# Constants, modulation set-up and the transposes of x as one list; four weight tiles of the merge on the ring's common slots

## The chip, the cores and the metric

The kernel runs on one core of one Trainium2 chip. The metric is the device time of one execution in microseconds (us), here the median of several executions. Everything is float32.

## The reference, cut to what matters

A transformer block over 512 tokens of width 1024, followed by two further layers and a small context stream. The part that the change touches is the input side of the first block: `x` is projected by one wide matrix `w_in`, four branches (three-scale window attention, indexed sparse attention, an RWKV-7 recurrence, a Mamba-2 scan) each give 256 columns, and these are merged under gates:

```
merged = sum over n of sigmoid(x @ w_gates[n]) * (branch_n @ w_branch[n])
y      = layer_norm(alpha * x + merged @ w_out)
```

Two sets of constants play a part. An identity matrix serves the transposes on TensorE. `na_mask` is a 16-wide window mask that the neighbourhood attention of the later layers reads. Beside the branches, the kernel computes the modulation of the later layers: `silu(c) @ w_ada + b_ada`, for two condition vectors `c` and `c_ctx`.

## The kernel before

**Stages.** The program is a sequence of blocks. A block gives each engine its own instruction list, and all engines meet at a barrier at its end. Most blocks are built by `products` (L233) from a list of groups. A group is a run of matmuls into one PSUM bank and the step that empties it on VectorE ("v"), ScalarE ("s") or GpSimd ("g"). Each engine works through its part of the list in the list's order, and `extra` adds instructions ahead of the list on SyncE and GpSimd.

**The start.** Three blocks follow one another. `layer_constants` (L545) builds the identity, ones, epsilons, the causal mask and the window mask on GpSimd. The window mask goes to DRAM and comes back spread over 128 partitions (L585, L587), and the block ends when it is back. `Ada.__init__` (L2666) then loads `c`, `c_ctx` and the bias `b_ada` on SyncE, fills `cs` and `pick` on GpSimd, and applies Silu on ScalarE; its block ends when `b_ada` has landed. `load_x` (L593) loads all of x (2 MB) in one transfer, behind it the first four weight tiles, and transposes x in eight groups of four 128x128 transposes into `xT`. The block after it (`branch_a_in`) starts with x times the first tile of `w_in`.

**Weights.** `Weights` (L167) holds the whole program's weight tiles, mostly 2 MB each, in one list in order of use. Each tile has a slot of a ring: `slots[i]` says how many slots tile i may choose from, and it takes the one whose last tile is oldest. `RING` is 4, `DEEP` is 5; slot 4 (`deep_ring_more`) exists only from the stage "deep" on, after the branches. `Weights.load` runs on SyncE in every `products` block. It issues transfers in the list's order, each behind a wait for the last group that used the slot before, and it stops at the first tile whose slot does not exist yet or whose slot's last user belongs to a later block:

```
            if self.slot[i] >= len(self.bufs):
                break
            if self.prior[i] is not None:
                if self.prior[i] not in self.last_group:
                    break
                sp.wait_ge(self.groups_done, self.last_group[self.prior[i]])
```

**The end of branch D and the merge.** The block `d_in` (in `branch_d`, L1463) multiplies x with the last tiles of the branches; the last four modulation tiles (`w_ada`) are used there too. Then come the convolution (`mamba_conv`), the block `d_rows` and the scan. A further block turns y into `oT`. The stage "deep" opens slot 4, and `merge` (L1770) starts. For each branch n it uses three tiles: two of the gates (`w_in`) and one of `w_branch`, 12 in all. The gates' product is made from seven half-size products (`seven`, L1835). Its first two (`one`, `two`) take x and the tiles as they are. The third needs a sum of rows of x (four `row_sums`, L1812, on VectorE) and a difference of weight columns (`right`, on VectorE, which waits for both tiles).

**Semaphores.** A stage that closes puts its semaphores on a list. When more than 100 are on it, `Signals.close` (L122) clears them all with instructions on GpSimd and all engines meet at one more barrier (L125, L126). This happens twice: after the convolution of branch D, and before the first layer of the second block.

## Time and profile before

| | |
|---|---|
| median of 3 runs | 4184.86 us (4181.7 to 4187.54) |
| profiled execution, its own time | 4185.21 us |
| its span, first to last instruction | 4183.3 us |
| TensorE (PE) busy | 3772.9 us, 90% of the span |
| VectorE (DVE) busy | 1747.9 us, 42% |
| ScalarE (ACT) busy | 759.7 us, 18% |
| GpSimd (POOL) busy | 170.5 us, 4% |
| mean granted TensorE clock | 0.945 of full speed |
| weights and data moved | 575.73 MB, mean 138 GB/s |

In the rows, PE is TensorE's matmuls and PEld its weight loads; SPq is a transfer issued by SyncE (SP), at the time of its issue; PEq, POOLq are the engines' sequencers. `L342` is a line of the kernel, often of a helper. "us to landing" is the time from a transfer's issue to its semaphore. An fp32 matmul over 512 columns appears as several records.

### The profile page before, as it was taken

How to read it: one execution, taken by the hardware profiler on the slowest of the kernel's cores; microseconds unless marked ns; L12 is line 12 of the kernel's file. 1: busy time of each engine (PE TensorE's matmuls, PEld its weight loads, DVE VectorE, ACT ScalarE, POOL GpSimd, SP SyncE). 2: the span in 40 equal slices, each digit the busy share in tenths (PEclk: the TensorE clock that was granted, in tenths of full speed). 3: DMA queues.
4: the chain of work that ended last, by engine and by line, in shares of the span. 5: the costliest groups of instructions: out<-in, count | busy, mean ns of one | idle time of the engine just before them, and what ended most of it. 6: DMA issues, size and time to landing. Idle time of an engine off the chain costs nothing. (4 is left out here: it accounts for less than half of the span.)

```text
span 4183.3 us, 38449 instructions
## 1 busy us (share of the span) xinstructions
PE 3772.9 (90%) x14796; PEld 2136.3 (51%) x14796; DVE 1747.9 (42%) x3047; ACT 759.7 (18%) x1696; POOL 170.5 (4%) x377
## 2 busy tenths in 40 slices
PE   7988777799878989999777999999998899999999
PEld 3653664444534435455433545458744555447844
DVE  0118743444523211111144555355446556345546
ACT  0212211111112201000122434010001354111000
POOL 1001000000010000000020200000000300000000
PEclk9989777799889999999988999999999999999999
DMA  7543001223266588888753110132222201122221
GB/s 294 180 160 112 1 4 51 91 101 122 93 245 271 205 331 352 343 340 343 309 190 107 41 61 21 71 111 81 81 81 86 103 21 61 61 81 81 81 81 60
DMA packets 197672, 575.73 MB, mean 138 GB/s; under 512 B 24548, under 2 KB 34580, under 8 KB 184232
## 3 DMA queue, kind: packets, MB, share of 16 engines
q1 hardware_dynamic: 177608, 517.31, 33.0%
q10 hardware_dynamic: 12000, 29.46, 2.0%
q0 software_dynamic: 7888, 26.53, 1.8%
q8 instruction: 120, 1.97, 0.2%
q14 instruction: 56, 0.46, 0.0%
HBM read 541.54 MB, written 31.73 MB: 137 GB/s over the span
## 5 line engine op out<-in xcount | busy, mean ns | idle before, releaser
L342 PE MATMUL ps<-out_sums 128*128 128x256 f32 (+1 forms) x1152 | 333.6, 450 | 2.3 <-issue 2.3
L342 PEld LDWEIGHTS ps<-out_sums 128*128 128x128 f32 x1152 | 218.7, 190 | 114.2 <-issue 94.5
L342 PE MATMUL ps<-mixers_xT,ring 128*128 128x512 f32 (+1 forms) x480 | 209.2, 594 | 0.9 <-PEq L272 0.9
L342 PE MATMUL ps<-ring,layers_hT 128*128 128x512 f32 x416 | 186.7, 607 | 21.8 <-PEq L126 11.3
L2262 PE MATMUL ps<-ring,mixers_xT 128*64 128x512 f32 x416 | 184.0, 599 | 3.8 <-issue 2.8
L2263 PE MATMUL ps<-ring,mixers_xT 128*64 128x512 f32 x416 | 186.5, 605 | 0.0
L342 PE MATMUL ps<-ring,out_hidden 128*128 128x512 f32 x384 | 167.4, 592 | 0.0
L342 PEld LDWEIGHTS ps<-mixers_xT,ring 128*128 128x128 f32 (+1 forms) x480 | 88.6, 187 | 115.8 <-issue 115.6
L342 PE MATMUL ps<-ring,deep_c_hT 128*128 128x512 f32 (+2 forms) x352 | 132.6, 534 | 11.8 <-PEq L272 11.0
L342 PEld LDWEIGHTS ps<-ring,layers_hT 128*128 128x128 f32 x416 | 79.6, 194 | 123.1 <-issue 119.1
L342 PE MATMUL ps<-out_hidden 128*128 128x512 f32 x288 | 125.7, 593 | 6.2 <-issue 6.2
L342 PE MATMUL ps<-layers_hT,ring 128*128 128x256 f32 x512 | 115.3, 387 | 5.1 <-ACT out_rms_rs L2592 5.1
L342 PEld LDWEIGHTS ps<-ring,out_hidden 128*128 128x128 f32 x384 | 73.0, 190 | 91.0 <-issue 90.9
L2262 PEld LDWEIGHTS ps<-ring,mixers_xT 128*64 128x64 f32 x416 | 56.2, 138 | 123.1 <-issue 123.1
L2300 DVE TENSOR_TENSOR moe_h<-moe_sg,ps 128x512 f32<-128x512 f32 x16 | 11.0, 688 | 253.4 <-PE ps L2263 253.4
L342 PE MATMUL ps<-ring,layers_yT 128*128 128x512 f32 x256 | 112.5, 592 | 0.0
L342 PEld LDWEIGHTS ps<-layers_hT,ring 128*128 128x128 f32 x512 | 99.4, 195 | 19.7 <-issue 5.5
L342 PE MATMUL ps<-ring,mixers_xT 128*128 128x512 f32 (+2 forms) x320 | 100.1, 470 | 8.0 <-DVE ab_qk L336 6.3
L342 PEld LDWEIGHTS ps<-ring,deep_c_hT 128*128 128x128 f32 x352 | 65.1, 193 | 77.0 <-issue 74.5
L430 PE MATMUL ps<-mla_kT,mla_qT 96*128 96x512 f32 (+1 forms) x256 | 96.8, 502 | 8.1 <-ACT mla_S L444 6.6
L342 PE MATMUL ps<-ring,ctx_ins 128*128 128x512 f32 (+1 forms) x232 | 98.1, 581 | 5.5 <-ACT ctx_ins L3239 3.3
L2262 PE MATMUL ps<-ring,moe_hT 128*64 128x512 f32 x192 | 88.0, 613 | 16.5 <-ACT moe_hT L334 7.6
(894 smaller groups left out, 6490.0 us busy)
## 6 DMA issues: line engine op xcount, KB each, us to landing
ring<-in_w_ff SPq DMA_DIRECT2D x44, 2048.0 KB
ring<-in_w_in SPq DMA_DIRECT2D x40, 2048.0 KB
ring<-in_e_up SPq DMA_DIRECT2D x27, 2048.0 KB
ring<-in_e_gate SPq DMA_DIRECT2D x25, 2048.0 KB
ring<-in_e_down SPq DMA_DIRECT2D x25, 2048.0 KB
ring<-in_w_ada SPq DMA_DIRECT2D x24, 2048.0 KB
ring<-in_w_out SPq DMA_DIRECT2D x8, 2048.0 KB
deep_ring_more<-in_e_gate SPq DMA_DIRECT2D x8, 2048.0 KB, 7.8
```

Source lines behind the costliest of these rows:

```text
L342: last = pe.matmul(out, lhsT, rhs, start=(j == 0), stop=(j == len(pairs) - 1))
L430: last = pe_.matmul(bank[:, e * BANK + c0:e * BANK + c0 + n], q, k, start=True, stop=True)
L2262: pe.matmul(bank[0:HALF, :], left(k)[:, 0:HALF], wa[:, k, cols], **ends)
L2263: last = pe.matmul(bank[HALF:P, :], left(k)[:, HALF:P], wb[:, k, cols], **ends)
L2300: lambda eng, bank, link, i=i: eng.tensor_tensor(h[:, i, :], sg[:, i, :], bank, ALU.mult),
```

## The change

1. The constants that the first blocks need, the modulation's set-up and the transposes of x become one block. SyncE's list is: x, then `c`, `c_ctx` and `b_ada` (two transfers), then the first four weight tiles. GpSimd makes the identity first and raises a semaphore `ident`, on which TensorE's first transpose waits beside `x_in`. The Silu becomes a group on ScalarE at the head of the list. GpSimd ends with a wait for `b_ada`.
2. x lands in `mixed` (the space of `oT`) and no longer in a buffer of its own.
3. The window mask is made in the block `branch_a_in`, behind the 16 zero-writes to `y_slot` that GpSimd issues there.
4. Of the merge's 12 tiles, the first four take their slot among the 4 common ones.

```
-        slots = [RING] * len(tiles)
+        slots = [RING] * (len(tiles) + RING)
...
-            with Stage(nc, "const") as sc:
-                layer_constants(M, sc)
...
 def load_x(M, st):
-    x_rows = st.sb("x_rows", [P, TT, D])
+    sig, ada = st.sig, M.ada
+    x_rows = M.mixed[:, :, :, :].rearrange("p i k n -> p (i k n)").rearrange("p (t d) -> p t d", t=TT)
 
     def sync(sp):
         sp.dma_start(x_rows[:, :, :], M.A["x"].rearrange("o (t p) d -> p (o t) d", p=P)
                      ).then_inc(sig["x_in"], 16)
+        ada.load(sp, M.A)
+
+    def constants(pool):
+        first_constants(M, st, pool)
+        ada.constants(pool)
+        pool.wait_ge(ada.sig["ada_b"], 16 * LAYERS)
...
     def first_pe(pe, bank):
+        pe.wait_ge(sig["ident"], 1)
         pe.wait_ge(sig["x_in"], 16)
         return first(pe, bank)
     gs[0].pe = first_pe
-    products(M, "xT", gs, extra={"sync": sync})
+    products(M, "xT", [group(None, ada.silu, "s")] + gs, extra={"sync": sync, "gpsimd": constants})
...
+            small = sa.sb("small", [WIN, 3, 2 * WIN])
...
                 for b in range(NE // 2, NBLK):
                     pool.dma_start(spare[b], z).then_inc(sa.sig["zeroed"], 16)
+                window_mask(M, small, sa.sig, pool)
                 pool.wait_ge(sa.sig["zeroed"], SPARE * 16)
...
+    def load(self, sp, A):
+        sp.dma_start(self.c[:, 0, :], A["c_2"]).then_inc(self.sig["ada_in"], 16)
+        sp.dma_start(self.c[:, 1, :], A["c_ctx_2"]).then_inc(self.sig["ada_in"], 16)
+        for l in range(LAYERS):
+            sp.dma_start(self.b[:, l, :], A["b_ada_2"][l]).then_inc(self.sig["ada_b"], 16)
...
+    def silu(self, act, _, link):
+        act.wait_ge(self.sig["ada_in"], 32)
+        act.wait_ge(self.sig["ada_zero"], 1)
+        return act.activation(self.cs[:, :, 0:2].rearrange("p k s -> p s k"), self.c[:, :, :], ACT.Silu)
```

`first_constants` and `window_mask` are the two halves of the old `layer_constants`; their instructions are the old ones.

SyncE at the start of the program. Before, two barriers and a wait for `b_ada` stand ahead of the transfer of x:

```order
L2675 UNCONDITIONAL_BRANCH [waits barrier_Pool_Activation_PE_DVE_SP_release]
L2677 DMA mixers_ada_c<-in_c 128x8
L2678 DMA mixers_ada_c<-in_c_ctx 128x8
L2680 DMA mixers_ada_b<-in_b_ada 128x48 x2
L2674 UNCONDITIONAL_BRANCH [waits mixers_ada_b]
L273 UNCONDITIONAL_BRANCH [waits barrier_Pool_Activation_PE_DVE_SP_release]
L599 DMA x_x_rows<-in_x 128x4x1024
L200 DMA ring<-in_w_in 128x8x512
L200 DMA ring<-in_w_ada 128x8x512 x2
L200 DMA ring<-in_w_in 128x8x512
```

And with the change:

```order
L273 UNCONDITIONAL_BRANCH [waits barrier_Pool_Activation_PE_DVE_SP_release]
L607 DMA mixers_oT<-in_x 128x4x1024
L2694 DMA mixers_ada_c<-in_c 128x8
L2695 DMA mixers_ada_c<-in_c_ctx 128x8
L2697 DMA mixers_ada_b<-in_b_ada 128x48 x2
L200 DMA ring<-in_w_in 128x8x512
L200 DMA ring<-in_w_ada 128x8x512 x2
L200 DMA ring<-in_w_in 128x8x512
```

x is the first transfer, and the four small ones stand between it and the first weight tile.

SyncE from the last tiles of `d_in` to the start of the merge, before:

```order
L200 DMA ring<-in_w_ada 128x8x512 [waits groups_done,d_conv_loads]
L200 DMA ring<-in_w_ada 128x8x512 [waits groups_done]
L272 UNCONDITIONAL_BRANCH
L273 UNCONDITIONAL_BRANCH [waits barrier_Pool_Activation_PE_DVE_SP_release]
L1537 DMA scratch_L<-ssm_dtl 4x512
L1539 DMA ssm_L_all<-scratch_L 128x2048 [waits xT_moved_v]
L272 UNCONDITIONAL_BRANCH [waits xT_moved_s]
L273 UNCONDITIONAL_BRANCH [waits barrier_Pool_Activation_PE_DVE_SP_release] x2
L200 DMA deep_ring_more<-in_w_in 128x8x512
L200 DMA ring<-in_w_in 128x8x512 [waits groups_done]
L200 DMA ring<-in_w_branch 128x2x1024 [waits groups_done]
L200 DMA ring<-in_w_in 128x8x512 [waits groups_done] x2
```

And with the change (the first of these rows is the second `w_ada` tile above):

```order
L200 DMA ring<-in_w_ada 128x8x512 [waits groups_done]
L200 DMA ring<-in_w_in 128x8x512 [waits groups_done] x2
L200 DMA ring<-in_w_branch 128x2x1024 [waits groups_done]
L200 DMA ring<-in_w_in 128x8x512 [waits groups_done]
L272 UNCONDITIONAL_BRANCH
L273 UNCONDITIONAL_BRANCH [waits barrier_Pool_Activation_PE_DVE_SP_release]
L1555 DMA scratch_L<-ssm_dtl 4x512
L1557 DMA ssm_L_all<-scratch_L 128x2048 [waits xT_chain_v]
L272 UNCONDITIONAL_BRANCH [waits xT_chain_s]
L273 UNCONDITIONAL_BRANCH [waits barrier_Pool_Activation_PE_DVE_SP_release] x2
L200 DMA deep_ring_more<-in_w_in 128x8x512
```

The merge's first four transfers have moved from the merge's block into `d_in`; only the fifth stands at the merge's start. From there on SyncE's list has the same transfers in the same order, with the tile that takes slot 4 moved by one (in each five, the fifth and no longer the first).

GpSimd where the semaphores are cleared for the first time, after the convolution's masks of branch D. Before:

```order
L1502 MEMSET d_conv_pre 128x4x3 [waits d_conv_masks]
L272 UNCONDITIONAL_BRANCH [waits d_conv_masks]
L125 ISA [waits barrier_Pool_Activation_PE_DVE_SP_gather]
L125 ISA x3
L322 UNCONDITIONAL_BRANCH [waits barrier_Pool_Activation_PE_DVE_SP_gather] x5
```

And with the change:

```order
L1520 MEMSET d_conv_pre 128x4x3 [waits d_conv_masks]
L272 UNCONDITIONAL_BRANCH [waits d_conv_masks]
L125 ISA [waits barrier_Pool_Activation_PE_DVE_SP_gather]
L125 ISA x5
L322 UNCONDITIONAL_BRANCH [waits barrier_Pool_Activation_PE_DVE_SP_gather] x5
```

The clearing has six instructions and no longer four; at the second place, before the second block's first layer, it has five and no longer four. Both places stay where they were.

## Rows read from the trace of the kernel before

**Rows 1.** The page, part 1: busy time, share of the span, instructions of each engine.

```profile
PE 3772.9 (90%) x14796; PEld 2136.3 (51%) x14796; DVE 1747.9 (42%) x3047; ACT 759.7 (18%) x1696; POOL 170.5 (4%) x377
```

**Rows 2.** Timeline, 0 to 28 us: start, duration, instruction, [idle before <-releaser].

```profile
0.81 0.20 POOL L554 MEMSET ident<- 128x128 f32 x1 [0.29 <-POOLq L4115]
...
7.43 0.55 POOL L587 DMA_DIRECT2D na_mask<-mask  x1 [1.39 <-DMA mask<-const_small]
...
10.95 0.90 SPq L2680 DMA_DIRECT2D mixers_ada_b<-in_b_ada  x2
...
13.65 0.39 SPq L599 DMA_DIRECT2D x_x_rows<-in_x  x1
14.09 0.50 SPq L200 DMA_DIRECT2D ring<-in_w_in  x1
...
21.70 5.48 PE L395 MATMUL ps<-ident,x_x_rows 128*128 128x128 f32 x32 [21.70 <-DMA x_x_rows<-in_x]
...
23.28 3.69 SPq L200 DMA_DIRECT2D ring<-in_w_in  x1
23.71 0.60 ACT L334 ACTIVATE mixers_xT<-ps 128x512 f32<-128x512 f32 x1 [11.36 <-PE ps L395]
...
28.12 27.71 PE L342 MATMUL ps<-mixers_xT,ring 128*128 128x512 f32 x64 [0.94 <-PEq L272]
```

**Rows 3.** Stretch after x has landed: ..., PEclk, DMA share, GB/s (last columns).

```profile
21.70:24.00 2.30, 2.30 (x11) 2.30 (x12) 0.69 (x1) 0.29 (x1) 0.00 (x0) 1.00 1.05 387
```

**Rows 4.** DMA issues: tensor, count, KB each, median us from issue to landing.

```profile
x_x_rows<-in_x SPq DMA_DIRECT2D x1, 2048.0 KB, 8.0
...
mixers_ada_b<-in_b_ada SPq DMA_DIRECT2D x2, 24.0 KB, 1.9
...
mixers_ada_c<-in_c SPq DMA_DIRECT2D x1, 4.0 KB, 1.8
mixers_ada_c<-in_c_ctx SPq DMA_DIRECT2D x1, 4.0 KB, 1.6
...
c_first_cols<-in_c_rk SPq DMA_DIRECT2D x1, 1.0 KB, 1.8
```

**Rows 5.** Timeline, end of d_in to the merge's first products.

```profile
684.07 1.95 PE L2717 MATMUL ps<-mixers_ada_pick,mixers_ada_rows 128*128 128x2 f32 x16
...
686.54 0.47 DVE L1556 TENSOR_SCALAR d_dt_s<-ssm_dt_raw,ssm_small 4x512 f32<-4x512 f32 x1 [0.32 <-PEq L272]
...
708.91 1.21 DVE L1580 TENSOR_TENSOR_SCAN ssm_dtl<-d_dt_one,d_dt_s 4x512 f32<-4x512 f32 x1
...
712.25 1.94 PE L395 MATMUL ps<-ident,ssm_xbc 128*128 128x128 f32 x8 [26.23 <-PEq L126]
...
762.70 1.94 PE L395 MATMUL ps<-ident,ssm_y 128*128 128x128 f32 x8 [8.33 <-PEq L1682]
...
765.59 1.22 DVE L1816 TENSOR_TENSOR merge_rows<-mixers_xT 128x1024 f32<-128x1024 f32 x1 [1.07 <-PEq L272]
...
766.59 3.44 SPq L200 DMA_DIRECT2D ring<-in_w_branch  x1
...
778.82 16.13 PE L342 MATMUL ps<-deep_ring_more,mixers_xT 128*128 128x512 f32 x32 [14.17 <-DMA ring<-in_w_in]
778.87 2.29 DVE L1863 TENSOR_TENSOR merge_right<-ring,deep_ring_more 128x2048 f32<-128x2048 f32 x1 [8.53 <-DMA ring<-in_w_in]
...
791.62 0.69 DVE L1881 TENSOR_TENSOR merge_sg<-merge_p,ps 128x512 f32<-128x512 f32 x1 [8.13 <-PE ps L342]
```

**Rows 6.** Stretches at the merge's start, columns as in rows 3.

```profile
778.00:783.00 5.00, 4.18 (x5) 1.85 (x6) 4.09 (x2) 0.00 (x0) 0.00 (x0) 0.50 1.03 395
...
783.00:784.00 1.00, 1.00 (x3) 0.38 (x2) 0.49 (x1) 0.00 (x0) 0.00 (x0) 0.94 1.05 385
```

**Rows 7.** Waits of PE, 1186 to 2090 us: total us, times, longest.

```profile
PE ps L2262 <- DMA deep_ring_more<-in_e_down: 5.7, 3, 2.5
...
PE ps L2262 <- DMA ring<-in_e_down: 3.7, 2, 2.3
```

More of the change, by code:

```diff
@@ new lines, in first_constants, with fill, keep @@
+def first_constants(M, st, pool):
+    link = Chain(pool, st.sig["made"])
+    def fill(ap, value):
+        link(pool.memset(ap, value))
+    def keep(ap, pattern, fill_value, op):
+        link(pool.affine_select(out=ap, in_=ap, compare_op=op, fill=fill_value, base=0, pattern=pattern,
+                                channel_multiplier=1))
+    fill(M.ident[:, :], 0.0)
+    keep(M.ident[:, :], [[-1, P]], 1.0, ALU.not_equal)
+    pool.sem_inc(st.sig["ident"], 1)
+    fill(M.ones[:, :], 1.0)
+    fill(M.eps[:, :], EPS)
+    fill(M.ln_eps[:, :], LN_EPS)
+    fill(M.causal[:, :], 0.0)
+    keep(M.causal[:, :], [[-1, P]], NEG, ALU.is_ge)
@@ new lines, in window_mask, with keep, window @@
+def window_mask(M, small, sig, pool):
+    nc, link = M.nc, Chain(pool, sig["windows"])
+    def keep(ap, pattern, base, cm, fill_value):
+        link(pool.affine_select(out=ap, in_=ap, compare_op=ALU.is_ge, fill=fill_value, base=base,
+                                pattern=pattern, channel_multiplier=cm))
+    link(pool.memset(small[:, :, :], 0.0))
+    def window(kind, c0, c1, low):
+        m = small[:, kind, c0:c1]
+        if low:
+            keep(m, [[1, c1 - c0]], c0, -1, NEG)
+        else:
+            keep(m, [[-1, c1 - c0]], WIN - 1 - c0, 1, NEG)
+    window(0, 0, 2 * WIN, True)
+    window(0, WIN + 8, 2 * WIN, False)
+    window(1, 0, 2 * WIN, True)
+    window(1, 0, 2 * WIN, False)
+    window(2, 0, 8, True)
+    window(2, WIN, 2 * WIN, False)
+    mask16 = nc.dram_tensor("mask16", [WIN, 6 * WIN], F32).ap()
+    pool.dma_start(mask16, small[:, :, :].rearrange("p a n -> p (a n)")).then_inc(sig["mask_out"], 16)
+    pool.wait_ge(sig["mask_out"], 16)
+    pool.dma_start(M.na_mask[:, :, :].rearrange("p a n -> p (a n)"),
+                   bass.AP(mask16.tensor, 0, [[6 * WIN, WIN], [0, ROWS], [1, 6 * WIN]])
+                   ).then_inc(sig["mask_in"], 16)
+    pool.wait_ge(sig["mask_in"], 16)
@@ new lines, in __init__, with constants @@
+        self.c, self.sig = st.sb("ada_c", [P, 2, DK]), sig
+    def load(self, sp, A):
[3 more added lines that the diff above has]
+            sp.dma_start(self.b[:, l, :], A["b_ada_2"][l]).then_inc(self.sig["ada_b"], 16)
+    def constants(self, pool):
+        link = Chain(pool, self.sig["ada_pool"])
+        pool.memset(self.cs[:, :, :], 0.0).then_inc(self.sig["ada_zero"], 1)
+        link(pool.memset(self.pick[:, :], 0.0))
+        for q in range(4):
+            link(pool.affine_select(out=self.pick[:, :], in_=self.pick[:, :], compare_op=ALU.not_equal,
+                                    fill=1.0, base=-32 * q, pattern=[[-1, 2]], channel_multiplier=1))
```

64 lines of the change are left out of this document (removed).

## The prediction

> **What bounds the kernel now.** I read the page first. TensorE is busy for 3772.9 us, 90% of the span [rows 1], and no other engine comes near; so a change counts only where it fills a stretch in which TensorE stands idle. Then I read the timeline at the two places that the diff touches. At the start the reader is to see that TensorE has no work for 21.70 us, and that what ends this wait is the transfer of x, issued only at 13.65 [rows 2]: two blocks of small work stand ahead of it, one up to about 10 us (the window mask's way through DRAM, last issue at 7.43), and one for the loads of c and b_ada. At the merge the reader is to see 14.17 us of idle TensorE that end with a weight tile [rows 5]. Behind both places the matmuls run densely, so time won there moves the rest of the program forward.
>
> **The start: x is issued earlier.** In the changed order the transfer of x is SyncE's first instruction behind the first barrier. The trace has no SyncE row there, but GpSimd's first constant behind the same barrier starts at 0.81 [rows 2], and I take this for SyncE as well. x then goes out 13.65 - 0.81 = 12.84 us earlier. It has an empty queue in both kernels, so it takes the same 8.05 us to TensorE's first transpose (21.70 - 13.65, 8.0 in the row of landings [rows 4]): the transposes start at 8.86. The identity costs nothing, since GpSimd makes it by about 1.5 us. The transposes and their emptying take as long as before, 28.12 - 21.70 = 6.42 us, so the first product with weights could start at 15.28. **-12.84 us.**
>
> **The start: what stands behind x.** Four small loads now lie between x and the first weight tile. The tile before was issued 0.44 us behind x. Its 2.1 MB at 387 GB/s [rows 3] take 5.4 us after x, which lands at 21.70, so it was there at about 27.1 to 27.2, some 0.9 us before 28.12, where TensorE asked for it. The cost of the small loads in a queue that is never empty is not in the trace. From below it is nothing, as they fit into those 0.9 us. From above: SyncE issues such loads 0.45 us apart (two in 0.90 [rows 2]), and the fifth of a series of 1 KB loads issued so still lands in 1.8 us [rows 4], so one keeps the queue for no more than 0.45 us; four make 1.8, less 0.9 of slack, 0.9 us. The issue of the block's last weight tile gives the same bound: it ended at 23.28 + 3.69 = 26.97, 1.1 us before the next block, and moves by at most 1.8. I take **+0.4 us**, the middle, as the ends are near each other. The rest is covered. The Silu waits for c, which lands within a microsecond or two behind x (at 9 to 11), and ScalarE's first emptying comes at 23.71 - 12.84 = 10.87; a Silu that is late by one microsecond is made up in the idle gaps between the four copies. GpSimd's wait for b_ada ends at about 11, four microseconds before the block does. Without this cover each microsecond would count in full.
>
> A rule of the Trainium skill speaks against this order. "DMA: Bandwidth & Descriptors", section "Measured (HBM→SBUF, 128 partitions, SWDGE, issued from GpSimd)", gives about 10.5 ns for each packet however small; four loads of 128 packets would then hold the queue for an estimated 5.4 us and not 1.8, and the sum below would end 4.1 us later. The rows on hand disagree: loads issued 0.45 us apart would pile up, and they do not.
>
> **The window mask** moves behind 16 zero-writes of GpSimd in the next block. That block is dense with matmuls (its first run is 27.7 us long [rows 2], and many follow), GpSimd has nothing else in it, and the mask is read only by the later layers: nothing.
>
> **The merge.** SyncE now issues the first four tiles in d_in, each behind the last group of a slot's previous user. Those are the third-last modulation tile, the last tile of w_in, and the two last modulation tiles, whose products end by about 684 us. All 7 MB at 387 GB/s are in by about 702, 60 us before use. The block that empties the transposes of y ends by 765.59 [rows 5], where VectorE starts on the merge; TensorE starts there too, not at 778.82. That is **-13.2 us** of its 14.17; 1 us is the barrier and stays. Is anything else late in its place? The first two products need only x and the tiles. The third needs a row sum and the first weight difference; VectorE's four sums last until 778.87 - 8.53 = 770.34 and two differences of 2.29 us end at 775, while TensorE comes to the third product only 16 us after its start, at 781.6, and VectorE's first emptying follows TensorE by 791.62 - 778.82 = 12.8 us, at 778.4. So nothing is late, and the merge stays bound by TensorE. The fifth tile is issued at 765.6 and is wanted for the second branch, as before.
>
> **What is put into d_in.** SyncE's last wait there is for the last modulation products, which end in PSUM at about 684.2; behind it one more issue. The block's other work goes on until 686.0 (684.07 + 1.95) and the next starts at 686.54 [rows 5]. An issue takes 0.4 us with room in the queue. At the merge's start, with two tiles issued, the third was held for 3.44 us [rows 5]; as much here would end at 688 and cost 1.3 us. In d_in the queue is emptier by then, so I take nothing, and keep 1.3. The transfers run on beside VectorE's convolution; VectorE's row sum and differences ran beside transfers at the merge too [rows 5], and I take it that nothing is stretched.
>
> **Clearing semaphores** has two more instructions at one place and one more at the other. Around the first place VectorE ends at 710.12 and TensorE starts at 712.25 [rows 5], 2.1 us. An ordinary barrier leaves 0.3 (686.54 [rows 5]), so four instructions and a second barrier take 1.8 us, at most 0.45 each. Three more cost 0 to 1.35 us; I take **+0.4**, since part of the 1.8 is the barrier.
>
> **The clock at the merge.** The granted clock was 0.50, the lower level of 1.2 GHz, until 783, 4.2 us after the products began [rows 6]. With the earlier start TensorE's eight transposes at 762.70 come just before. I let the clock rise 4.2 us after the start of the products again: nothing. If the transposes count, it rises at about 766.9, and 2.9 us of half speed are saved, 1.45 us.
>
> **Slots from there on.** The merge and the experts rotate through five slots in both kernels, each tile waits for the user five tiles back, and SyncE's order is the same: nothing.
>
> **Sum.** -12.84 + 0.4 - 13.2 + 0.4 = -25.2 us. The profiled execution took 4185.21 us, so 4160.0 us; it stands 0.35 above the median of the three runs shown, which is no difference.
>
> **The rivals.**
> - *The small loads hold the queue.* In the worst case each takes its whole landing time in turn: 1.8 + 1.6 + 1.9 + 1.9 = 7.2 us [rows 4], less 0.9 of slack, 6.3 and not 0.4. The time would be 4165.9. Against it is the series that did not pile up; for it, that none was ever behind a full queue. 0.09. The packet rule of "DMA: Bandwidth & Descriptors" in the Trainium skill would land between this and the forecast, at 4164.1.
> - *The transposes count for the clock.* 4160.0 - 1.45 = 4158.5. For it: they are TensorE work less than a microsecond before the products. Against: the whole scan, with TensorE busy, left the clock low. 0.10.
> - *Only one of the two halves pays.* At the merge, tiles issued early don't help if a second wait was hidden behind the first; then 4160.0 + 13.2 = 4173.2. The same size results if x, as the program's very first transfer, came 12 us late. The order of SyncE speaks against the first, landings of 1.6 to 1.8 us for the first transfers of the program against the second. 0.06.
> - *Slower: the shifted fifth slot starves the experts.* There weights arrive only just in time: TensorE waits for e_down in five places, 9.4 us in all, at most 2.5 us each [rows 7]. If the shift made one tile of each of the 16 pairs of experts late by those 2.5 us, it would cost 40 us: 4200. It turns slower by over 8.4 us from 33.6 / 16 = 2.1 us a pair. Against it: each tile still waits for the user five tiles back, in the same order. 0.02.
> - *The change doesn't do what it says*: tiles held until the merge's block. The listed order excludes it for the merge, and x is first in its list. No chance of its own.
>
> **How the numbers follow.** The forecast has 0.73. A measurement of this kernel can tell about 0.2% from no change, 8.4 us, here below 4176.5 us. All cases but the last and a remainder for the unforeseen lie below that: faster 0.97, same 0.01, slower 0.02. The bounds of the costs: at best -12.84 - 13.2 - 1.45 = -27.5 (4157.7), at worst -12.84 + 0.9 - 13.2 + 1.3 + 1.35 = -22.5 (4162.7). The runs shown scatter by 3 us to either side, and the rival with the held queue is taken in: 4155 to 4167 us.
>
> **What would show it.** In the new profile: x issued near 0.8 and the first transpose near 8.9; the first weight product at 15.3 to 16.2, with a wait for the ring if the small loads cost something; the next block of GpSimd at the same time. The block d_in should be followed by the convolution about 12.4 us earlier than before, at 674, and not later; the merge's first product at about 753.5, with 1 us of idle before it and no wait for a tile; from there to the end every stage some 25 us earlier. A wait of TensorE for w_in at the merge, or more than 9.4 us of waits for e_down, would show me wrong; so would a first transpose later than 10 us.

## The result, and the profile after

| | before | changed |
|---|---|---|
| median, first measurement | 4186.2 us (4181.7 to 4191.12, 4 runs) | 4161.9 us (4157.03 to 4166.67, 4 runs) |
| ratio, 95% interval | | 0.9945 [0.9932, 0.9957] |
| median, second measurement (below, *after_again*) | 4184.47 us (4179.93 to 4194.59, 11 runs) | 4155.87 us (4154.18 to 4164.43, 6 runs) |
| ratio, 95% interval | | 0.9933 [0.992, 0.9946] |
| profiled execution | 4185.21 us, span 4183.3 | 4163.72 us, span 4160.9 |

The kernel is faster by 0.55% and 0.67%, 24 and 29 us. The forecast was 4160.0 with a range of 4155 to 4167.

The page after, part 1, answers to [rows 1]: the work is the same, and TensorE's busy time has not shrunk but grown by 4.1 us, within a span shorter by 22.4.

```profile
PE 3777.0 (91%) x14796; PEld 2137.9 (51%) x14796; DVE 1747.7 (42%) x3047; ACT 758.7 (18%) x1696; POOL 170.5 (4%) x377
```

The start of the changed kernel, from the timelines of SyncE, TensorE and ScalarE (start, duration, instruction, idle before); it answers to [rows 2].

```profile
0.81 0.44 SPq L607 DMA_DIRECT2D mixers_oT<-in_x  x1
...
3.38 0.46 SPq L200 DMA_DIRECT2D ring<-in_w_in  x1
...
10.89 3.71 SPq L200 DMA_DIRECT2D ring<-in_w_in  x1
...
9.13 5.50 PE L395 MATMUL ps<-ident,mixers_oT 128*128 128x128 f32 x32 [9.13 <-DMA mixers_oT<-in_x]
15.57 27.71 PE L342 MATMUL ps<-mixers_xT,ring 128*128 128x512 f32 x64 [0.94 <-PEq L272]
...
9.39 0.23 ACT L2710 ACTIVATE mixers_ada_cs<-mixers_ada_c 128x16 f32<-128x16 f32 x1 [4.75 <-DMA mixers_ada_c<-in_c_ctx]
...
14.67 0.60 ACT L334 ACTIVATE mixers_xT<-ps 128x512 f32<-128x512 f32 x1 [0.28 <-PE ps L395]
```

x goes out at 0.81 and the first product with weights starts at 15.57 and not at 28.12: 12.55 us won. The idle before it is the barrier's 0.94 in both kernels, so no weight tile was late. What ends this block is ScalarE: its last emptying of a transpose ends at 15.27 (14.67 + 0.60), and the product follows 0.30 us later. Before the change it was the same, with the last emptying at 27.82 and the product at 28.12:

```profile
27.22 0.60 ACT L334 ACTIVATE mixers_xT<-ps 128x512 f32<-128x512 f32 x1 [0.27 <-PE ps L395]
```

SyncE's last weight load was issued at 14.60 (10.89 + 3.71), 0.67 us before ScalarE was done.

From the clearing of the semaphores to the merge, the timelines of TensorE, SyncE and VectorE; they answer to [rows 5].

```profile
696.31 1.21 DVE L1598 TENSOR_TENSOR_SCAN ssm_dtl<-d_dt_one,d_dt_s 4x512 f32<-4x512 f32 x1
...
699.94 1.94 PE L395 MATMUL ps<-ident,ssm_xbc 128*128 128x128 f32 x8 [26.51 <-PEq L126]
...
750.25 1.94 PE L395 MATMUL ps<-ident,ssm_y 128*128 128x128 f32 x8 [8.33 <-PEq L1700]
753.28 15.80 PE L342 MATMUL ps<-ring,mixers_xT 128*128 128x512 f32 x32 [1.09 <-PEq L272]
...
669.91 0.37 SPq L200 DMA_DIRECT2D ring<-in_w_branch  x1
671.63 0.37 SPq L200 DMA_DIRECT2D ring<-in_w_in  x1
...
753.09 0.38 SPq L200 DMA_DIRECT2D deep_ring_more<-in_w_in  x1
...
765.76 0.69 DVE L1899 TENSOR_TENSOR merge_sg<-merge_p,ps 128x512 f32<-128x512 f32 x1 [3.35 <-PE ps L342]
```

The third and fourth tile of the merge are issued in d_in, the fifth at the merge's start, and the merge begins with 1.09 us of idle time in place of 14.17: 25.54 us ahead of before. Two stretches show the clock there, as [rows 6] did; the columns are the busy times of PE, PEld, DVE, ACT and POOL, then the granted clock, the DMA share and GB/s.

```profile
756.00:757.00 1.00, 1.00 (x3) 0.48 (x2) 1.00 (x2) 0.00 (x0) 0.00 (x0) 0.52 1.05 408
757.00:758.00 1.00, 1.00 (x4) 0.47 (x3) 1.00 (x2) 0.00 (x0) 0.00 (x0) 1.00 1.05 406
```

To see what became of the lead, I took the start of the same SyncE instruction in each kernel, less its start in the kernel before:

| instruction (its start before, us) | after | after_again | start_only | slots_only | warm_timed | halves |
|---|---|---|---|---|---|---|
| load of c_first_cols (316.0) | -12.62 | -12.72 | -11.67 | -1.23 | -12.04 | -8.53 |
| load of c_out_gw (607.3) | -13.07 | -13.12 | -12.55 | -1.15 | -12.43 | -10.48 |
| load of ctx (1030.2) | -25.86 | -26.08 | -12.28 | -14.49 | -27.55 | -23.83 |
| second load of ctx (1170.2) | -25.98 | -25.92 | -14.39 | -14.55 | -27.24 | -23.49 |
| e_up for ctx_ins (2084.9) | -24.49 | -31.93 | -15.38 | -12.71 | -28.07 | -29.15 |
| load of ctx_h (2129.1) | -25.17 | -32.40 | -15.00 | -10.21 | -28.54 | -28.54 |
| mla_rope (2218.8) | -23.15 | -30.57 | -14.77 | -8.42 | -26.40 | -29.86 |
| na_gains (3426.3) | -22.81 | -29.97 | -14.80 | -8.03 | -25.78 | -30.88 |

Each step stands out in the columns of the kernels that have it, and so does something else: between 1170 and 2219 us the executions gain or lose up to 6.4 us of their own. In the profiled execution of the changed kernel it was a loss of nearly 3.

### The profile page after: what moved, and what is told of

The parts are those of the page before. It is cut to its first block and busy times, and to the rows that moved or that the text cites. A ratio compares the mean times of both kernels' runs of the same rounds, so it can differ in the third digit from the quotient of the medians.

```text
span 4160.9 us, 38434 instructions
## 1 busy us (share of the span) xinstructions
PE 3777.0 (91%) x14796; PEld 2137.9 (51%) x14796; DVE 1747.7 (42%) x3047; ACT 758.7 (18%) x1696; POOL 170.5 (4%) x377
## 5 line engine op out<-in xcount | busy, mean ns | idle before, releaser
L342 PE MATMUL ps<-ring,deep_c_hT 128*128 128x512 f32 (+1 forms) x320 | 138.6, 591 | 12.1 <-PEq L272 11.1
L342 PE MATMUL ps<-ring,ctx_ins 128*128 128x512 f32 (+1 forms) x272 | 113.4, 576 | 5.2 <-ACT ctx_ins L3251 3.3
L2280 PE MATMUL ps<-ring,moe_hT 128*64 128x512 f32 x208 | 96.9, 621 | 14.6 <-ACT moe_hT L334 10.3
## 6 DMA issues: line engine op xcount, KB each, us to landing
ring<-in_w_ff SPq DMA_DIRECT2D x45, 2048.0 KB, 12.8
ring<-in_w_in SPq DMA_DIRECT2D x41, 2048.0 KB, 11.3
```

The costliest lines, as they stand in the source:

```text
L342: last = pe.matmul(out, lhsT, rhs, start=(j == 0), stop=(j == len(pairs) - 1))
L2280: pe.matmul(bank[0:HALF, :], left(k)[:, 0:HALF], wa[:, k, cols], **ends)
```

## The experiments

The theory: two stretches of idle TensorE, 12.84 us at the start and 13.2 at the merge, were removed and add up, and nothing else changed. The rivals: small loads that hold the queue, only one half that pays, a shifted ring that starves the experts.

### One half at a time

**start_only**, the changed kernel with the old slots:

```diff
-        slots = [RING] * (len(tiles) + RING)
+        slots = [RING] * len(tiles)
```

> The change without its fourth part: the merge's tiles wait for the stage deep as before. Theory (two independent gains): only the start pays, 12.5 us, 0.3 us of it given back where the semaphores are cleared, so 4186.2 - 12.3 = 4173.9 us; TensorE idle 14.2 us for w_in at the merge. Rival (the start's gain is partly lost later, e.g. to the clock or the slots): if the 3.4 us that the changed kernel's profile lost between the merge and the end are lost here too, with the slots of before, the slots are not their cause, and the time is nearer 4177. Rival (one half alone pays nothing): 4186.

**slots_only**, the kernel before with the new slots:

```diff
-        slots = [RING] * len(tiles)
+        slots = [RING] * (len(tiles) + RING)
```

> The kernel before with the fourth part alone. Theory: 13.1 us from TensorE's start on the merge (about 765.7 and not 778.8), the clearing unchanged with four instructions (2.1 us between VectorE's scan and TensorE's transposes, not 2.4), so 4186.2 - 13.1 = 4173.1 us. Rival (early tiles only uncover a second wait, or disturb d_in): 4180 or more, with the block after d_in later than 686.5. Rival (the shifted fifth slot costs time in the experts): more waits of TensorE for e_down than 9.4 us.

Measured: start_only 4170.71 us (4167.04 to 4176.65, 8 runs), ratio 0.9967 [0.9957, 0.9978]; slots_only 4173.23 us (4168.12 to 4177.03, 7 runs), ratio 0.9966 [0.9955, 0.9978]; the kernel before had 4187.62 beside them. The merge in start_only and in slots_only, TensorE's timeline of each:

```profile
765.59 17.07 PE L342 MATMUL ps<-deep_ring_more,mixers_xT 128*128 128x512 f32 x32 [14.10 <-DMA ring<-in_w_in]
```

```profile
764.61 15.83 PE L342 MATMUL ps<-ring,mixers_xT 128*128 128x512 f32 x32 [1.09 <-PEq L272]
```

With the old slots the wait of 14 us is back, with the new ones it is gone. Each half saves a third of a per cent, and 0.33 + 0.34 = 0.67% is what the whole change saves in its second measurement and lies just inside the interval of the first. That only one half pays is refuted. start_only's median lies 3.2 us under what I had expected and slots_only's 0.1 over; both are within the 9 to 10 us by which their runs scatter.

### How many tiles must go early

**one_early** and **two_early** give the common slots to one and to two tiles instead of four (`RING` in the first diff replaced by 1 and by 2).

> One tile early. Theory: the first product waits for both gate tiles, so the second one, issued at 753.1 and alone in the queue, ends the wait after its 5.4 us at 387 GB/s and about 2 us until its semaphore: TensorE idle 7 to 9 us, the time 6 to 8 us over the changed kernel. Rival (a product can start on one tile): 1 us of idle. Rival (the wait is a fixed cost of the stage's opening, not of the bytes): 14 us.

> The change with two tiles on the common slots and not four. Theory: the merge's first products need only the two gate tiles, w_branch is wanted 23 us later, so TensorE starts at 753.3 as in the changed kernel, with 1.1 us of idle, and the time is the same (4162). Rival (all four are needed): an idle of 3 us or more at the merge, or a wait for w_branch after 16 to 40 us.

Measured: one_early 4164.32 us, two_early 4160.84, one execution each. TensorE's timeline at the merge of one_early, then of two_early:

```profile
762.39 15.44 PE L342 MATMUL ps<-ring,mixers_xT 128*128 128x512 f32 x32 [8.72 <-DMA deep_ring_more<-in_w_in]
```

```profile
756.47 16.74 PE L342 MATMUL ps<-ring,mixers_xT 128*128 128x512 f32 x32 [1.09 <-PEq L272]
```

With one early tile TensorE is idle for 8.72 us, with two for the barrier's 1.09: the third and fourth are in time even if issued at the merge's start. The wait is what the trace of before said it was, the landing of the second tile.

But the rows show something more. The 32 matmuls of one_early read `ring`, the first tile, and wait for `deep_ring_more`, the second. The second tile isn't read by them at all; the program makes them wait, since `seven` names both tiles in every one of its products (cut from the kernel, `wa` is the first tile, `wb` the second):

```
    b11, b12, b21, b22 = wa[:, 0:half, :], wb[:, 0:half, :], wa[:, half:DK, :], wb[:, half:DK, :]
...
                     ev, on, max(ta, tb), other=min(ta, tb), needs=needs, after=after)
...
    one = pair(a11, b11, lambda act, bank, link, x: act.activation(p1[x], bank, ACT.Copy), "s", (), lambda x: old[x])
    two = pair(a12, b21, c11, "v", (), lambda x: (one[x], *old[x]))
```

A kernel whose products `one` and `two` wait for the first tile alone would have some 16 us of work while the second one lands. It was not run; it could make one early tile enough, or shorten the wait without any.

As times of whole executions the two say little. two_early's merge began at 756.47 and not at the expected 753.3, but the delay was there before: at the mark 607 it led by 9.15 us, where the changed kernel led by 13.07. one_early was expected 6 to 8 us over the changed kernel; it took 2.4 us more than the first median and 8.5 more than the second.

### Small loads behind x

**more_small**: b_ada comes in eight transfers instead of two, so ten small loads lie between x and the first weight tile instead of four.

```diff
-            sp.dma_start(self.b[:, l, :], A["b_ada_2"][l]).then_inc(self.sig["ada_b"], 16)
+            for c in range(0, 6 * DK, 12):
+                sp.dma_start(self.b[:, l, c:c + 12], A["b_ada_2"][l][:, c:c + 12]).then_inc(self.sig["ada_b"], 16)
```

> b_ada in eight transfers of 128 packets and not two, behind x: ten small loads ahead of the first weight tile, not four. Theory (a small load holds the queue for no more than the 0.3 us that four cost together, under 0.45 each): the first product comes at most 6 x 0.45 = 2.7 us later than 15.57, less what slack is left, and the issues of SyncE, 0.45 us each, end by 6.1 us, before x has landed. Rival (a small packet costs as in the packet rule of the Trainium skill, DMA: Bandwidth & Descriptors, about 10.5 ns each): 768 more packets put the first product 8 us later, at about 23.

Measured: 4156.55 us. SyncE's and TensorE's timelines of more_small:

```profile
2.31 4.05 SPq L2698 DMA_DIRECT2D mixers_ada_b<-in_b_ada  x8
6.40 0.43 SPq L200 DMA_DIRECT2D ring<-in_w_in  x1
...
11.77 5.11 SPq L200 DMA_DIRECT2D ring<-in_w_in  x1
...
17.33 29.24 PE L342 MATMUL ps<-mixers_xT,ring 128*128 128x512 f32 x64 [2.38 <-PEq L272]
```

Six more loads move the first product from 15.57 to 17.33. Here it is SyncE that ends the block: ScalarE's last emptying ends at 15.58, SyncE's last weight load is issued at 16.88 (11.77 + 5.11), 2.28 us later than in the changed kernel, and the product follows 0.45 us behind. What the six loads took of the transfers' time is less. The stretches from 8 to 11 us, more_small first and then the changed kernel (columns as above):

```profile
8.00:11.00 3.00, 1.97 (x10) 2.00 (x11) 0.69 (x1) 0.23 (x1) 0.00 (x0) 1.00 1.12 259
```

```profile
8.00:11.00 3.00, 1.87 (x9) 1.90 (x10) 0.69 (x1) 0.23 (x1) 0.00 (x0) 1.00 1.07 371
```

259 GB/s in place of 371 for 3 us are 0.34 MB that didn't come, an estimated 0.9 us at 387 GB/s, or 0.15 us a load. By the packet rule of the Trainium skill ("DMA: Bandwidth & Descriptors", section "Measured (HBM→SBUF, 128 partitions, SWDGE, issued from GpSimd)", about 10.5 ns a packet) six loads of 128 packets should hold the queue for an estimated 8 us. The trace doesn't agree with that for loads issued by SyncE: an estimated 0.9 us of transfers and 2.3 us of SyncE's time.

The wait has a longer tail than its 1.44 us of new idle time (2.38 less 0.94): the products behind it took 29.24 us instead of 27.71. That is the clock. The stretches from 18 to 20 us, again more_small and then the changed kernel:

```profile
18.00:20.00 2.00, 2.00 (x3) 0.67 (x2) 0.00 (x0) 0.00 (x0) 1.42 (x8) 0.50 1.03 380
```

```profile
18.00:20.00 2.00, 2.00 (x6) 0.82 (x5) 0.00 (x0) 0.00 (x0) 1.58 (x3) 1.00 1.06 388
```

All profiles of this document agree on it. In nine of them TensorE is idle for 0.94 us ahead of the first 64 products, and these take 27.70 or 27.71 us. In the other five (more_small, pieces, mask_at_start, halves, best) it is idle for 2.38 to 5.07 us, the granted clock falls to 0.50, and they take 29.24 to 29.92 us. So a block that ends late here costs its delay and another 1.5 to 2.2 us. That more_small's whole execution was none the slower shows how little a single time tells about such sums here.

### What ends the first block

**mask_at_start** puts the window mask back into GpSimd's first block:

```diff
         pool.wait_ge(ada.sig["ada_b"], 16 * LAYERS)
+        window_mask(M, small, st.sig, pool)
```

> The window mask back in the first block, behind the constants. Theory: its two trips through DRAM run beside 8 MB of loads from other queues, each 4 to 8 us with the engines full, so GpSimd ends at 15 to 22 us and holds the block's barrier for up to 6 us over 15.5. Rival (the mask is hidden wherever it stands): the first product at 15.6 as in the changed kernel.

Measured: 4172.8 us. GpSimd's and TensorE's timelines:

```profile
12.45 0.54 POOL L594 DMA_DIRECT2D na_mask<-mask  x1 [4.59 <-DMA mask<-x_small]
...
18.15 29.40 PE L342 MATMUL ps<-mixers_xT,ring 128*128 128x512 f32 x64 [4.00 <-PEq L272]
```

The mask's trip through DRAM now runs beside x and the weights; its last transfer is issued at 12.45, and TensorE starts at 18.15, 2.58 us later than in the changed kernel. I put this down to GpSimd's wait for that transfer: it took 5.0 us to land, up to 17.5, while SyncE had issued its last load at 14.59 and ScalarE had emptied the last transposes at 14.79. So moving the mask out was a needed part of the change and not a neutral one: in the changed kernel GpSimd waits 23.0 us for the same mask in the next block, and nobody waits for GpSimd. The products behind took 29.40 us, 1.69 more, at the low clock. Its lead was 6.55 us at the mark 316 and 4.08 at the mark 607, where the changed kernel had 12.62 and 13.07. Of these 9.0 us, 4.3 are the delay and the clock at the start. The 2.5 us that it lost between the two marks need not be the mask's, as two_early, with the mask where the changed kernel has it, lost 2.2 us there. The rest stays open; it is one execution.

**pieces** tries to start the transposes earlier: x in four column transfers, then only the first 128 columns of the first weight tile, everything else in the next block, and Silu last.

```diff
-        sp.dma_start(x_rows[:, :, :], M.A["x"].rearrange("o (t p) d -> p (o t) d", p=P)
-                     ).then_inc(sig["x_in"], 16)
+        x = M.A["x"].rearrange("o (t p) d -> p (o t) d", p=P)
+        for c in range(4):
+            cols = slice(c * D // 4, (c + 1) * D // 4)
+            sp.dma_start(x_rows[:, :, cols], x[:, :, cols]).then_inc(sig[f"x_in{c}"], 16)
...
+        M.weights.load_first(sp)
...
-    products(M, "xT", [group(None, ada.silu, "s")] + gs, extra={"sync": sync, "gpsimd": constants})
+    products(M, "xT", gs + [group(None, ada.silu, "s")], extra={"sync": sync, "gpsimd": constants, "hold": True})
```

> The change with x in four transfers by columns, each pair of transpose groups waiting for its own, the first 128 columns of the first weight tile right behind, the rest of it and the other tiles from the next block on, and the Silu last on ScalarE's list. Theory (the start is bound by the bytes of x in the queue, then by TensorE): transposes begin at about 4.5 us, the last two groups at about 9.2, the first product at 11 to 12.5 us and not 15.57: 3 to 4.5 us less than the changed kernel. Rival (narrow rows of 1 KB and 512 B slow the queue): x lands at 11 or later and the gain is gone. Rival (later tiles come late, since they are issued in the next block): a wait for the ring within the first 60 us.

Measured: 4178.64 us (4172.95 to 4186.03, 11 runs), ratio to before 0.9989 [0.998, 0.9998]: nearly all of the gain is gone. The timelines of TensorE, ScalarE and SyncE:

```profile
4.96 3.65 PE L403 MATMUL ps<-ident,mixers_oT 128*128 128x128 f32 x16 [4.96 <-DMA mixers_oT<-in_x]
9.43 3.66 PE L403 MATMUL ps<-ident,mixers_oT 128*128 128x128 f32 x16 [0.82 <-DMA mixers_oT<-in_x]
15.57 29.40 PE L350 MATMUL ps<-mixers_xT,ring 128*128 128x512 f32 x64 [2.48 <-PEq L279]
...
48.23 1.92 PE L2739 MATMUL ps<-ring,mixers_ada_cs 128*32 128x512 f32 x16 [1.40 <-DMA ring<-in_w_ada]
59.59 9.38 PE L350 MATMUL ps<-mixers_xT,ring 128*128 128x512 f32 x16 [9.44 <-DMA ring<-in_w_in]
...
13.74 1.28 ACT L2726 ACT_TABLE_LOAD   x1
15.04 0.23 ACT L2726 ACTIVATE mixers_ada_cs<-mixers_ada_c 128x16 f32<-128x16 f32 x1
...
15.53 0.38 SPq L202 DMA_DIRECT2D ring<-in_w_in  x1
```

Two things went wrong. The transposes are done at 13.09, but Silu is last and needs a table of its own, whose load takes 1.28 us; the block ends with it at 15.27, by chance the very time at which ScalarE ends it in the changed kernel. After 2.48 us of idle time the clock falls here too (29.40 us for the 64 products). And the big loads go out only at 15.53, after a queue that had run dry. From 26 to 60 us the transfers run at 412 to 416 GB/s, in the changed kernel at 401 to 418, and no faster; what the queue stood idle comes back as waits of 1.40 and 9.44 us for tiles at 48 and 59. At the load of c_first_cols, at 316 us in the kernel before, this kernel is 4.71 us behind it, where the changed kernel leads by 12.62.

**halves** mends both: x in two halves, all loads left in the first block, Silu in the middle.

```diff
-        sp.dma_start(x_rows[:, :, :], M.A["x"].rearrange("o (t p) d -> p (o t) d", p=P)
-                     ).then_inc(sig["x_in"], 16)
+        x = M.A["x"].rearrange("o (t p) d -> p (o t) d", p=P)
+        for c in range(2):
+            cols = slice(c * D // 2, (c + 1) * D // 2)
+            sp.dma_start(x_rows[:, :, cols], x[:, :, cols]).then_inc(sig[f"x_in{c}"], 16)
...
-    products(M, "xT", [group(None, ada.silu, "s")] + gs, extra={"sync": sync, "gpsimd": constants})
+    products(M, "xT", gs[:4] + [group(None, ada.silu, "s")] + gs[4:],
+             extra={"sync": sync, "gpsimd": constants})
```

> The changed kernel with x in two column halves instead of one transfer, all weight loads left in the first block and Silu between the two sets of transposes. Theory (x in pieces lost because the queue stood empty while the weight loads waited for the first block's end, not because of the pieces): the marks at 316 and 607 us stand 12 to 14 us ahead of before, as in the changed kernel, the first four transpose groups begin at 6 to 7.5 us, the first product waits for the weight tile if that lands after 14.5 us, and no wait for a weight tile at 48 and 59 us. Rival (pieces with rows of 2 KB and 512 B cost transfer rate, so x's last column is late): the second set of transposes begins after 10 us and the first product after 16 us.

Measured: 4154.97 us. SyncE's and TensorE's timelines:

```profile
9.34 7.57 SPq L200 DMA_DIRECT2D ring<-in_w_in  x1
...
6.42 6.20 PE L395 MATMUL ps<-ident,mixers_oT 128*128 128x128 f32 x32 [6.42 <-DMA mixers_oT<-in_x]
17.35 29.92 PE L342 MATMUL ps<-mixers_xT,ring 128*128 128x512 f32 x64 [4.74 <-PEq L272]
```

The waits for tiles at 48 and 59 us are gone, as the theory has it. But its marks are not: I expected a lead of 12 to 14 us at 316 and 607, and it has 8.53 and 10.48. The transposes, which now end at 12.62, two microseconds earlier, bring nothing: the first product starts 1.8 us later than in the changed kernel, and behind the idle 4.74 us the low clock stretches the 64 products by 2.2 us more. Together that is 4.0 of the 4.1 us by which it is behind the changed kernel at the mark 316. The first weight tile was there at 14.9 (issued at 4.19, 10.7 us to landing). What was not there is SyncE. It could issue its fourth weight load only from 9.34 to 16.91, and the block ends with it; the product follows 0.44 us later. In more_small the same sum is 16.88 and 17.33, 0.45 apart. One more transfer (halves) and six more (more_small) both held the last issue 2.3 us longer than in the changed kernel, so this isn't a price by the load; what the queue waits for isn't in these rows. In both the start is bound by **the issue of the block's last load into a full queue**. In the changed kernel it is not yet: with the same 0.44 us behind the issue at 14.60 the product could have started at 15.04, and ScalarE held it until 15.57. So SyncE had 0.53 us in hand, and 2.28 less 0.53 is the 1.76 us of more_small. The likely remedy, halves with that fourth load moved into the next block, was not run; in the changed kernel the first tile lands at 14.7 (issued at 3.38, 11.3 us to landing), so at most 0.9 us of 15.57 is to be had.

halves has one more difference. It has one more semaphore, and both places at which semaphores are cleared moved: TensorE starts 0.52 us behind VectorE's scan and not 2.42, and the barrier of the clearing now stands before the convolution, 2.02 us of idle VectorE in place of 0.32. pieces and best have it too. The sum is nearly the same, but a comparison between marks from there on is not clean.

### The clock at the merge

**warm** has four products whose result is thrown away ahead of the block that empties y, where TensorE stands idle for 8.3 us; **warm_timed** is the same kernel in several executions.

```diff
+        @block.tensor
+        def _(pe):
+            for _ in range(4):
+                pe.matmul(M.ps[:, 7, :], M.ident[:, :], M.xT[:, 0, :], start=True, stop=True)
```

> The change with four extra products of the identity and a row of x in TensorE's idle time while VectorE works on branch D's y (their result is not used). Theory (the clock is low because TensorE did little before): the granted clock is high when the transposes of y start, these take 1.0 us and not 1.9, and the merge starts warm, so that its first 32 products take 14 us and not 15.8: 2 to 3 us less at the merge. Rival (the products run past VectorE's work and delay the transposes): up to 1 us lost. Rival (the clock falls in the gap again): nothing.

> The changed kernel with four products of idle TensorE (ident by the block's own xT, result thrown away into bank 7) ahead of the mamba block's transposes, timed. One look gave 4160.03 us and a merge that began its products 2.3 us earlier. Theory (TensorE at the merge starts at the low level and the four products take that time while it waits anyway): 2 to 2.5 us under the changed kernel, ratio between the two about 0.9995, perhaps inside the scatter. Rival (the gained time is lost again in the waits of the next blocks): the same time as the changed kernel within 0.5 us at the mark 1170.

TensorE's timeline of warm_timed:

```profile
743.77 5.44 PE L1704 MATMUL ps<-mixers_xT,ident 128*128 128x512 f32 x8 [0.84 <-PEq L1620]
751.26 1.06 PE L395 MATMUL ps<-ident,ssm_y 128*128 128x128 f32 x8 [2.05 <-PEq L1700]
753.42 13.97 PE L342 MATMUL ps<-ring,mixers_xT 128*128 128x512 f32 x32 [1.09 <-PEq L272]
```

The transposes take 1.06 us instead of 1.94 and the first 32 products 13.97 instead of 15.80: all of the low clock at the merge is gone. From the mark 607 to the mark 1030 warm_timed gains 2.2 us on after_again, as the theory said (2 to 2.5). The lead of 1.5 us over after_again at the mark 1030 is 1.3 at the mark 1170, so it is not lost in the waits behind. In the measured time it can't be seen: warm (one execution) 4160.03; warm_timed 4156.58 us (4153.27 to 4159.9, 5 runs), ratio 0.9928 [0.9915, 0.9942], beside 0.9933 [0.992, 0.9946] of the changed kernel.

**best** joins halves and warm.

> Both of the above together: x in two halves and the four idle products at the merge. Theory: the gains add, so 2 to 4 us under the changed kernel (ratio to the kernel before 0.992 to 0.994). Rival (the start is bound by transfers: about 400 GB/s from 5 to 53 us, so that a product begun earlier only waits for a tile later): the halves bring nothing and the time is that of the warmed kernel within 1 us.

Measured: 4164.56 us (4161.51 to 4169.72, 5 runs), ratio 0.9949 [0.9935, 0.9963]. It is no better than the changed kernel, perhaps worse. Neither expectation came true: the gains don't add, and the time isn't that of warm_timed within 1 us but 8 us over it. At the start the halves cost about as much as in halves alone (17.13 and 29.66 us for the 64 products; 5.1 us behind the changed kernel at the mark 316), and its lead is 5.11 us at the mark 607; the merge is warm (13.97 us). None of my versions is shown to beat the changed kernel.

### The microseconds between the marks

**after_again** is the changed kernel once more.

> The changed kernel once more, beside its rivals of this call. Theory (both halves pay their full gain, 12.5 us at the start and 13.1 us at the merge, and what single executions give back or gain later is the granted clock's drift after short idles): a ratio of 0.993 to 0.995 to the kernel before, and a profiled execution whose marks stand 25 to 26.5 us ahead of those before up to 1900 us, with a later loss of 0 to 5 us at other places than in the first one. Rival (the 3.4 us lost between 2039 and 2184 us belong to the new slots): the same loss, 3 to 4 us, at the same two places again.

Measured: 4155.87 us, ratio 0.9933 [0.992, 0.9946]. Up to the mark 1170 its execution follows the first within 0.3 us (the table above). Then it gains 6 us where the first lost 1.5. The same instructions in both, first the changed kernel's first execution, an expert's products with e_down at 2023 us and the products behind ckv; then after_again, TensorE's timeline of each:

```profile
2022.88 0.62 PE L2280 MATMUL ps<-ring,moe_hT 128*64 128x512 f32 x1
...
2023.31 1.05 PE L2280 MATMUL ps<-ring,moe_hT 128*64 128x512 f32 x1
...
2026.70 0.61 PE L2280 MATMUL ps<-ring,moe_hT 128*64 128x512 f32 x1
...
2138.01 8.80 PE L342 MATMUL ps<-ring,norm_in_c_ckvT 128*128 128x512 f32 x16 [2.62 <-issue]
```

```profile
2018.14 0.59 PE L2280 MATMUL ps<-ring,moe_hT 128*64 128x512 f32 x1
...
2018.57 0.59 PE L2280 MATMUL ps<-ring,moe_hT 128*64 128x512 f32 x1
...
2130.86 7.11 PE L342 MATMUL ps<-ring,norm_in_c_ckvT 128*128 128x512 f32 x16 [2.61 <-issue]
```

The same program, after the same idle gap of 2.6 us, needs 8.80 us in one execution and 7.11 in the other for the same 16 products. The granted clock of the stretches says why, for 2138 us in the first and 2130.9 in the second:

```profile
2138.00:2142.00 4.00, 3.99 (x7) 1.72 (x8) 3.93 (x4) 0.97 (x3) 0.00 (x0) 0.67 1.04 403
```

```profile
2130.90:2134.90 4.00, 4.00 (x10) 1.85 (x11) 3.93 (x4) 1.30 (x5) 0.00 (x0) 1.00 1.03 401
```

So at these two places, 2023 and 2138, the lead was given back by the clock, which after a short gap sometimes falls for some microseconds and sometimes doesn't, and not by the slots: in one program the loss is there once and missing once. The rest isn't settled by that. Between the marks 2129 and 2219 the table has a loss of 1.8 to 2.1 us in all of after, after_again, warm_timed and slots_only, as the rival has it, and two_early, mask_at_start and warm have it as well. The kernel before, start_only and one_early, with no and with one early tile, don't have it. That speaks for the slots. The gain of 1.3 us of halves doesn't speak against them, since there the clearing of the semaphores has left this stretch: TensorE is idle for 29.7 us in it and not for 32, and busy for 58.7 us, 57.0 before. What does is more_small, with the slots and the blocks of the changed kernel and 0.1 us of loss. In after_again the loss lies at another place than in the first execution, in the 32 transposes of norm_in_yg, which took 6.57 us there, 5.92 in the first execution and 5.05 before. It is TensorE's own pace each time and never a wait for a tile; that it is the clock is argued and not shown, and up to 2 us that the new slots cost at this place stay possible. The experts didn't starve. The waits for e_down in the changed kernel, answering to [rows 7]:

```profile
PE ps L2280 <- DMA ring<-in_e_down: 7.0, 4, 2.4
...
PE ps L2280 <- DMA deep_ring_more<-in_e_down: 2.4, 1, 2.4
```

9.4 us in all as before, in five places; after_again had 6.8 us in four, warm_timed 11.0 in six, and with one half each start_only had 8.5 and slots_only 8.5.

## Why the prediction was right

- **x issued earlier, -12.84.** As read: 0.81 in place of 13.65. It landed 8.3 us after its issue, not 8.05, so the transposes started at 9.13 and not at 8.86.
- **Small loads, +0.4 (0 to 0.9).** The term came out near, but not by its mechanism. The first product came 0.29 us later than a shift by 12.84 would give, and 0.27 of that is x's own later landing; with ten small loads behind it instead of four x took no longer (8.22 us in more_small). SyncE's last issue moved by 12.37 us (26.97 to 14.60) and not by 12.84, so the four loads cost it 0.47 us, and 0.53 of slack covered them. The transposes and ScalarE's emptying ended the block, as I had it, with SyncE's issue as the second bound. The rival with 6.3 us and the packet rule between it and the forecast are both refuted, by this and by more_small.
- **The transposes as long as before.** 5.50 us in place of 5.48, and here the profiled execution was kind. Over the nine profiles in which ScalarE's emptying ends this block the same 32 transposes took 5.39 to 6.68 us, at a granted clock of 1.00, and in the seven of them with the new start the first product came between 15.52 and 16.49. Why stays open. Up to a microsecond of the start's agreement is luck.
- **The window mask, nothing.** Right where the change puts it. mask_at_start shows what the cover was worth: in the first block it costs 2.58 us and another 1.69 by the clock.
- **The merge, -13.2.** Idle time fell from 14.17 to 1.09, 13.1 us, and VectorE's first emptying came 12.5 us behind the start, as forecast (12.8). one_early and two_early show that it hangs on the second tile alone. That the first two products need both tiles is how the program waits and not what they read; the forecast had no use for the difference.
- **What is put into d_in, nothing (up to 1.3).** The last issue took 0.37 us, at 671.63; VectorE's next block began at 673.95, 12.59 us earlier than before. Nothing.
- **Clearing semaphores, +0.4 (0 to 1.35).** From the end of VectorE's scan at 697.52 to TensorE's start at 699.94 it is 2.42 us, 2.13 before: +0.29 for the two instructions of the first place. The kernels with six instructions there have 2.41 or 2.42 in all nine profiles, slots_only with four has 2.12. For the one more instruction of the second place nothing can be seen.
- **The clock at the merge, nothing (rival: -1.45).** It rose 3.7 us after the products began, 4.3 before. The transposes didn't count; that rival is refuted.
- **Slots from there on, nothing.** No more waits for e_down in the changed kernel (9.4 and 6.8 us). The slower rival with its 40 us is refuted, and the one with one half by the two experiments. A cost of up to 2 us between 2129 and 2219 is not excluded.

By these terms the merge should begin 12.84 - 0.4 + 13.2 - 0.4 = 25.2 us earlier. It began 25.54 earlier. What the sum left out is what comes behind: I let the rest of the program move forward unchanged for 3400 us. It drifts: between the marks 1170 and 3426 the executions of the table move by -7.4 to +6.5 us. The two medians, 4161.9 and 4155.87, lie on both sides of 4160.0, so the sum was right within what this kernel's measurement can tell, and no closer.

## What to carry to other kernels

A wait of the busiest engine that ends with a transfer is worth its whole length if the transfer can be issued in an earlier block, but only as many tiles as the first products wait for have to go early; count them before giving up buffers, and see whether the products read all that they wait for. A block ends with the last of its engines, the one that empties and the one that issues loads among them: look at when the last load could be issued into the full queue, since an earlier start of the work gains nothing past that point. A block that ends late can cost more than its delay, if TensorE's clock falls while it waits. And where a stretch is bound by transfers, never let the queue run dry for the sake of an earlier first product; it comes back as waits, here 11 us for transposes that ended 1.5 us earlier and gained nothing.

## What the runs showed of the hardware

- The clock's fall after a short gap isn't always reproducible from one execution to the next: 7.11 or 8.80 us for the same 16 products after the same 2.6 us, and single products of an expert at 1.05 in place of 0.59 for 3.4 us in one of the two executions. By the marks, these two drift 7 us apart.
- At the start it was reproducible: after 0.94 us of idle TensorE the first 64 products took 27.70 or 27.71 us (nine profiles), after 2.38 to 5.07 us, with the granted clock down to 0.50, 29.24 to 29.92 us (five profiles).
- Four throwaway products of 128x512 in an idle stretch of TensorE raised the clock ahead of the merge: the first 32 products took 13.97 us in place of 15.80.
- The issue of a 2 MB load on SyncE took 0.37 us with room in the queue and 3.66 to 7.57 us as the last of the first block, 10.31 us in pieces; one small change ahead of it (one transfer more, or six) cost the same 2.3 us.
- Small loads of 128 packets each, issued by SyncE amid 2 MB loads, took an estimated 0.15 us each of the transfers' time (by six more of them, 259 and 371 GB/s over 3 us).
- Two more instructions that clear semaphores cost 0.29 us.
- The order of two kinds of activation decides how many tables are loaded: with Silu first one load of 1.28 us served it and the copies, with the copies first (halves, pieces) Silu needed a second one of 1.28 us, which counts in full if it comes last.
